# Feed-forward input projection: one pass of 512 columns per rounded weight tile, with the second half copied out by ScalarE

## The reference, cut to what matters

```
h   = rms_norm(x, norm_ffn_g)
a, b = split(h @ ffn_w_in)          # 1024 x (2 * 2816)
x   = x + (silu(a) * b) @ ffn_w_out # 2816 x 1024
```

## Time and profile before

| | |
|---|---|
| median of three runs | 1561.72 us (1561.06 to 1565.51) |
| profiled execution, its span | 1557.4 us |
| median less span | 4.3 us |
| instructions | 28378 |
| busy: TensorE, VectorE, ScalarE | 98%, 76%, 49% of the span |
| share of the closing chain on TensorE | 85% |
| input projection, first to last matmul | 291.2 to 418.3 us |

### The profile page before, as it was taken

The page is one execution under the profiler, slowest core; times in us unless marked ns, Lnnn a source line. Parts: engine busy times, 40 slices in busy tenths (PEclk is TensorE's granted clock), DMA queues, the critical chain, the costliest instruction groups (busy, mean ns, idle before and its releaser), DMA issues.

```text
span 1557.4 us, 28378 instructions
## 1 busy us (share of the span) xinstructions
PE 1530.9 (98%) x10460; PEld 1384.1 (89%) x10460; DVE 1180.4 (76%) x2029; ACT 766.8 (49%) x1089; POOL 60.5 (4%) x108
## 2 busy tenths in 40 slices
PE   8999999999999999999999999999999999999997
PEld 7768897999999887989999999999998888888886
DVE  7996645776636968757699999988865777777776
ACT  5237544544435563425444654645545445444544
POOL 2002000100000034000000000000000000000000
PEclk9999999999999999999999999999999999999999
DMA  7363668455533230516287777555557777777773
GB/s 303 115 259 137 243 241 314 155 184 190 186 112 114 83 109 9 200 49 244 86 228 219 226 225 216 173 165 153 164 157 245 236 239 240 237 242 237 240 243 123
DMA packets 95940, 293.64 MB, mean 189 GB/s; under 512 B 10480, under 2 KB 45424, under 8 KB 82928
## 3 DMA queue, kind: packets, MB, share of 16 engines
q1 hardware_dynamic: 95712, 292.21, 57.1%
q10 hardware_dynamic: 144, 0.26, 0.0%
HBM read 274.60 MB, written 17.83 MB: 188 GB/s over the span
## 4 chain that ended last, share of the span: by engine, by line
PE 85%; DVE 9%; DMA 2%; ACT 1%; issue 1%; SPq 0%; DVEq 0%; POOL 0%; ACTq 0%; POOLq 0%
PE ps L467 85%; DVE big L1518 1%; DVE split_ring L2120 1%; DMA ring<-in_peer_v 1%; DVE big L1543 1%; DMA ring<-in_peer_u 1%; DMA kept_acts<-acts 1%; DVE big L1425 0%; DVE big L2169 0%; DVE big L2173 0%; DVE big L2171 0%; DMA kept_acts<-par 0%; DVE big L1981 0%; DMA x<-in_x 0%; DVE big L1501 0%
## 5 line engine op out<-in xcount | busy, mean ns | idle before, releaser
L467 PE MATMUL ps<-split_hh,split_ring 128*128 128x256 f32 x3392 | 423.2, 284 | 3.6 <-DVE split_ring L2120 3.0
L467 PEld LDWEIGHTS ps<-split_hh,split_ring 128*128 128x128 f32 x3392 | 412.0, 192 | 5.7 <-DVE split_ring L2120 2.3
L467 PE MATMUL ps<-split_ring 128*128 128x512 f32 (+1 forms) x1712 | 386.9, 384 | 3.0 <-DVE split_ring L2120 2.7
L467 PEld LDWEIGHTS ps<-split_ring 128*128 128x128 f32 x1712 | 313.4, 188 | 69.0 <-DVE split_ring L2120 6.6
L2120 DVE TENSOR_TENSOR split_ring<-ring,split_ring 128x1024 fp32r<-128x1024 f32 x256 | 311.7, 1220 | 49.4 <-ACT split_ring L2720 47.3
L2727 ACT ACTIVATE split_ring<-ring 128x1024 fp32r<-128x1024 f32 x128 | 135.8, 1062 | 172.2 <-DMA ring<-in_peer_v 172.1
L2720 ACT ACTIVATE split_ring<-ring 128x1024 fp32r<-128x1024 f32 x128 | 135.2, 1057 | 93.9 <-DMA ring<-in_peer_u 93.8
L467 PE MATMUL ps<-split_ffn_h,split_ffn_w 128*128 128x256 f32 x1056 | 127.4, 283 | 0.0
L467 PEld LDWEIGHTS ps<-split_ffn_h,split_ffn_w 128*128 128x128 f32 x1056 | 127.0, 192 | 0.1
L2229 DVE TENSOR_TENSOR split_ring<-ring,split_ring 128x256 fp32r<-128x256 f32 x128 | 54.4, 425 | 80.4 <-ACT split_ring L2734 80.3
L1726 DVE TENSOR_TENSOR split_ffn_w<-ring,split_ffn_w 128x2048 fp32r<-128x2048 f32 x33 | 75.6, 2291 | 49.8 <-ACT split_ffn_w L2520 49.8
(11 more groups left out here) (348 smaller groups left out, 1895.1 us busy)
## 6 DMA issues: line engine op xcount, KB each, us to landing
ring<-in_peer_u SPq DMA_DIRECT2D x128, 512.0 KB, 4.1
ring<-in_peer_v SPq DMA_DIRECT2D x128, 512.0 KB, 3.6
ring<-in_w_mod SPq DMA_DIRECT2D x24, 1024.0 KB, 5.9
ring<-in_ffn_in SPq DMA_DIRECT2D x22, 1024.0 KB, 4.9
ring<-kept_acts SPq DMA_DIRECT2D x128, 128.0 KB, 3.3
ring<-in_ffn_out SPq DMA_DIRECT2D x11, 1024.0 KB, 4.9
ring<-in_w_out SPq DMA_DIRECT2D x8, 1024.0 KB, 9.0
ring<-in_peer_wq SPq DMA_DIRECT2D x8, 1024.0 KB, 7.6
```

The source lines that it names most:

```text
L467: return nc.tensor.matmul(out, lhsT, rhs, start=start, stop=stop, skip_group_check=True)
```

## The change

Blocks 1 to 21 have one pass of 512 columns where two passes of 256 stood. The rounded weights move `split["ffn_h"][:, :, k, :]`, the high and the low part of the input side by side; the low weights still move the high part alone, into the left 256 columns. Gate and value get a bank each, blocks alternate between bank pairs 0, 1 and 2, 3 outside the planner's turn, and each block waits for block `j - 2` to be taken. The right halves (high weights by low input) are copied to SBUF by ScalarE (`copy_right`), then VectorE adds left and copy, then multiplies by the inverse. Block 0 keeps its 48 matmuls of 256. `ctx_sum` goes to an upper bank, with `after("ctx_sum")` behind it on TensorE, and its square root is placed at the end of ScalarE's turn 1.

```
+        right = h[:, 0:4, :].rearrange("p (n m) t -> p n m t", m=2)
...
+        def ffn_banks(j):
+
+            return ps[:, 2 * (j % 2):2 * (j % 2) + 2, :]
...
-            def total(key, parts, takers=("act",), n=T, ones_=None):
-
-                bank = begin(key, *takers)
+            def total(key, parts, takers=("act",), n=T, ones_=None, upper=0):
+
+                bank = begin(key, *takers, upper=upper)
...
             for j in range(FB):
-                bank = begin(("ffn", j), "dve")
+                if j >= 2:
+                    after(("ffn", j - 2))
+                for b in (2 * (j % 2), 2 * (j % 2) + 1):
+                    if j < 2 and plan.in_bank[b] is not None:
+                        after(plan.in_bank[b])
+                    plan.in_bank[b] = ("ffn", j)
+                plan.add(("ffn", j), ("act", "dve") if j else ("dve",), banked=False)
+                both = ffn_banks(j)
                 weights("ffn_in", j)
                 high, low = (w[:, j % 3, :].rearrange("p (m k c) -> p m k c", m=2, k=KD) for w in (fw_high, fw_low))
                 pe.wait_ge(w_split, len(first_items) + j + 1)
...
+                if j == 0:
...
+                else:
                     for m in range(2):
                         for k in range(KD):
-                            if j == 0 and n == 0 and m == 0:
-                                pe.wait_ge(flag("ffn_h_high_ready"), k + 1)
-                            last = mm(bank[:, m * T:(m + 1) * T], w[:, m, k, :], rhs[:, k, :],
-                                      n == 0 and m == 0 and k == 0, n == 2 and k == KD - 1)
+                            mm(both[:, m, :], high[:, m, k, :], split["ffn_h"][:, :, k, :], k == 0, False)
+                        for k in range(KD):
+                            last = mm(both[:, m, 0:T], low[:, m, k, :], fh_high[:, k, :], False, k == KD - 1)
                 last.then_inc(made, 1)
                 release()
                 if j == 1:
                     pe.wait_ge(flag("squares_folded"), 1)
-                    total("ctx_sum", [sq[:, 0, :]])
+                    total("ctx_sum", [sq[:, 0, :]], upper=1)
+                    after("ctx_sum")
...
             for j in range(FB):
-                bank = s.product(("ffn", j))
                 both = f_both[:, j % 2]
-                s.took(("ffn", j), v.tensor_tensor(both, bank.rearrange("p (a t) -> p a t", a=2), both_r, ALU.mult))
+                dve.wait_ge(made, number(("ffn", j)))
+                left = ffn_banks(j)[:, :, 0:T]
+                if j:
+                    s.after(("ffn", j), "act")
+                    s.took(("ffn", j), v.tensor_tensor(both, left, right[:, j % 2], ALU.add))
+                    s.after(("ffn", j), "dve")
+                    v.tensor_tensor(both, both, both_r, ALU.mult).then_inc(flag("ffn_normed"), 1)
+                else:
+                    last = v.tensor_tensor(both, left, both_r, ALU.mult)
+                    s.took(("ffn", j), last)
+                    s.after(("ffn", j), "dve")
                 if j:
                     hidden_low(j - 1)
                 ffn_low(j + 3)
...
+            def copy_right(j):
+
+                if j == 1:
+                    s.wait("ffn_h_split")
+                if j >= 3:
+                    s.after(("ffn", j - 2), "dve")
+                act.wait_ge(made, number(("ffn", j)))
+                s.took(("ffn", j), a_(right[:, j % 2], ffn_banks(j)[:, :, T:], ACT.Copy))
+
             for j in range(FB):
-                if j == 2:
-                    std_of("ctx_sum", D, T, 1)
                 ffn_high(j + 3)
-                s.after(("ffn", j), "dve")
+                if j:
+                    s.wait("ffn_normed", j)
+                else:
+                    s.after(("ffn", j), "dve")
                 gate = f_both[:, j % 2, 0, :]
                 a_(gate, gate, ACT.Silu).then_inc(flag("silu_ready"), 1)
                 s.wait("hid_ready", j + 1)
                 a_(hid_high[:, j, :], hid[:, j, :], ACT.Copy).then_inc(flag("hid_high_ready"), 1)
+                if j == 1:
+                    std_of("ctx_sum", D, T, 1)
+                if j + 1 < FB:
+                    copy_right(j + 1)
```

More of the change, by code:

```diff
@@ L891, in _ @@
                 pe.wait_ge(w_split, len(first_items) + j + 1)
-                for n, (w, rhs) in enumerate(((high, fh_high), (low, fh_high), (high, fh_low))):
-                    if j == 0 and n == 2:
-                        pe.wait_ge(flag("ffn_h_split"), 1)
+                if j == 0:
+                    for n, (w, rhs) in enumerate(((high, fh_high), (low, fh_high), (high, fh_low))):
+                        if n == 2:
+                            pe.wait_ge(flag("ffn_h_split"), 1)
+                        for m in range(2):
+                            for k in range(KD):
+                                if n == 0 and m == 0:
+                                    pe.wait_ge(flag("ffn_h_high_ready"), k + 1)
+                                last = mm(both[:, m, 0:T], w[:, m, k, :], rhs[:, k, :], n == 0 and k == 0,
+                                          n == 2 and k == KD - 1)
+                else:
                     for m in range(2):
                         for k in range(KD):
-                            if j == 0 and n == 0 and m == 0:
-                                pe.wait_ge(flag("ffn_h_high_ready"), k + 1)
-                            last = mm(bank[:, m * T:(m + 1) * T], w[:, m, k, :], rhs[:, k, :],
-                                      n == 0 and m == 0 and k == 0, n == 2 and k == KD - 1)
+                            mm(both[:, m, :], high[:, m, k, :], split["ffn_h"][:, :, k, :], k == 0, False)
+                        for k in range(KD):
+                            last = mm(both[:, m, 0:T], low[:, m, k, :], fh_high[:, k, :], False, k == KD - 1)
                 last.then_inc(made, 1)
```

## The result

The changed kernel takes 1569.81 us at the median of seven runs (1567.15 to 1572.45), against 1561.72 for the kernel before (seven runs, 1559.98 to 1565.51). The ratio is 1.0044, 95% interval 1.0031 to 1.0057: slower, by 8.1 us (0.44%) between the medians. The profiled execution is the fastest of the seven, 1567.15 us, with a span of 1565.2, 7.8 above the span before.

What follows compares the result with a forecast made beforehand. The prediction took TensorE, busy 98% of the span, as the bound. Its terms, 1.7 + 7.4 + 1.7 + 2.3 - 4.3 = +8.8 us, took the span from 1557.4 to 1566.2; plus 4.3 gave 1570.5 us, range 1565.8 to 1575.5.

Steps and rivals of the forecast that it cites:

- wait before block 0: Before the projection, TensorE waits for ScalarE to take `ffn_sum` from bank 0: 1.7 us more.
- wait behind `ctx_sum`: After block 1, TensorE waits for ScalarE's square root of `ctx_sum`, at the end of its turn 1: 7.4 us more.
- clock behind it: After the `ctx_sum` wait, TensorE's first matmuls run slow, priced like the kernel's start: 1.7 us more, bounds 0 and 3.4.
- wait behind block 4: Block 7 waits for VectorE to take block 5, delayed by its 7.52 us norm of `ctx`: 2.3 us more.
- wide pass: Blocks 1 to 21: 512-column matmuls at 227.3 ns replace pairs at 240.0, saving 4.3 us; bounds 0 and 9.0.
- The 4.3 us put on top of the span: Whole kernel: the median of the runs was taken to stand 4.3 us above the profiled span.
- The rival in which the clock stays up: Behind the `ctx_sum` wait, no slow matmuls: 1.7 us less, 1568.8 us; chance 0.14.
- The two rivals on it, nothing and 9.0 us: Projection blocks 1 to 21: wide pass saves nothing, 1574.8 us, chance 0.08; or saves 9.0 us, 1565.8 us, chance 0.06.
- The loop: Projection's cycle of copy, rounding, low weights, hidden product and rounding: 5.43 us a turn, just under TensorE's 5.56.
- the rival that makes it the bound: From block 8 on, the copy, rounding and hidden-product loop sets the pace: 1571.8 to 1573.7 us; chance 0.14.

Runs made afterwards that it cites:

- the filler: Changed kernel with 31, then 15, float32 matmuls that nobody reads put into TensorE's wait behind `ctx_sum`; 1578.60 and 1572.99 us, one run each.
- the run with two copies: Kernel with all three waits gone, but ScalarE does each copy of a right half twice; 1560.22 us, one run, stage 128.26 us.
- 15 fillers: Changed kernel with 15 float32 matmuls that nobody reads behind `ctx_sum`, ending before the square root; 1572.99 us, one run.
- 31 fillers: Changed kernel with 31 float32 matmuls that nobody reads behind `ctx_sum`, running past the square root's end; 1578.60 us, one run.
- the kernel with the narrow passes: Kernel with all three waits gone, but each wide pass undone into two of 256 columns, copy and add kept; 1562.13 us, ratio to before 0.9996.

## Why the prediction was right

The time, 1569.81, lies in the range, 0.7 us under the forecast of 1570.5, and slower as forecast. Term by term, with the runs' values in the stage:

| term | forecast, us | measured, us | from |
|---|---|---|---|
| wait before block 0 | +1.7 | +1.72 | start of the projection, 2.50 after the sum against 0.78 |
| wait behind `ctx_sum` | +7.4 | +7.36 | 312.08 - 304.48 less 0.24 before (303.14 - 302.90) |
| clock behind it | +1.7 | +1.96 | block 2's copy, 7.92 against 5.96 us |
| wait behind block 4 | +2.3 | +2.08 | first matmuls of blocks 6 and 8, 349.82 - 336.56, less two blocks of 5.59 |
| block 0's own matmuls | none | -0.09 | 5.85 against 5.94 us, by first matmuls |
| wide pass | -4.3 | -3.63 | stage of 124.48 against 128.11 |
| sum | +8.8 | +9.40 | the stage, measured whole: +9.38 |

That the time came nearer to its forecast than this sum did is in part luck. The stage was 0.6 us longer than forecast, while the work behind it took 1.7 us less than before in the profiled execution (1137.2 against 1138.9), which no run traces to the change. The 4.3 us put on top of the span is no fixed cost either: the changed kernel's profiled run took 1.9 us more than its span (1567.15 against 1565.2), and the rest of the 4.6 us up to its median is that this run was the fastest of seven.

*The waits.* All three stood where the prediction put them, ended by the instructions it named. The walk through the times was good to 0.1 us for the first two, because each of their steps was in the trace of before: TensorE ran past the same square roots there, and their ends could be read off. The third is 0.2 us short of the forecast, since TensorE is ready for block 7 that much later. The prediction let block 0 of the kernel before last 5.76 us and so had ScalarE begin 0.45 us after the end of a block; by the first matmuls block 0 lasted 5.94 us (to 297.14), and ScalarE began 0.26 us after it. The rest is that a block takes 5.59 and not 5.56 us.

*The clock.* I had read the lower level from the pace of the first matmuls after the start, against a granted clock of 1.00 in the earlier trace rows. In the changed kernel the column itself shows 0.50 behind the long wait, and the filler takes the fall away. Its price, 1.96 us, is near the 1.7 borrowed from the start, but it is not fixed: with the bank pairs swapped the same wait was followed by a block 2 that was 0.6 us faster. The rival in which the clock stays up is refuted for this wait. The Trainium skill, "TensorE: Matmul & The Clock Gate", part 1, "The HAM clock gate", has the throttled state as default with activity as its release; the stretches of 0.50 after the wait and of 1.00 with the filler agree.

*The wide pass.* Mis-sized by 0.7 us: the term used 227.3 ns for a wide matmul and 240.0 for a pair, 12.7 saved; the runs give 10.8, a wide matmul of 229.2 ns. The two rivals on it, nothing and 9.0 us, are both refuted. By the Trainium skill, "TensorE: Matmul & The Clock Gate", "Back-to-back issue gap", whose formula is for a matmul by itself, the change would have saved 2.5 ns a pair; the measurement decides for 10.8.

*The loop.* Back to back it takes 353.44 - 348.03 = 5.41 us in the changed kernel, where 5.43 was forecast (copies of blocks 6 and 7):

```profile
348.03 0.58 ACT L2575 ACTIVATE hh<-ps 128x512 f32<-128x512 f32 x1
...
353.44 0.58 ACT L2575 ACTIVATE hh<-ps 128x512 f32<-128x512 f32 x1
```

It stays 0.18 us under TensorE's block, so the rival that makes it the bound did not come in; the run with two copies shows that it would have, and at the place and price that its arithmetic gives.

*Where it was less sure than it looked.* The prediction added up one profile. The three waits stood in every profile that has them, but the clock's falls did not (below), and the forecast had only one. The waits removed one by one give back 8.5, 2.2 and 2.1 us, 12.8 in all; the three together 13.0. The parts nearly add up.

## What to carry to other kernels

A product that is taken out late costs nothing while nobody needs its bank, and everything once the busiest engine waits for it by name: before placing a wait on that engine, read from the trace when the thing waited for ends, and ask whether a later wait already covers it. With fewer banks in rotation a long block of work on the draining engine, here one norm of 7.5 us, can become a gap on TensorE. Widening the moving operand is worth its 10.8 ns a pair only where these waits are kept off; with them gone the same change is 0.41% faster than the kernel before, of which the stage shows 3.63 us, 0.23%.

## What the runs showed that I had not expected

Short waits can drop TensorE's clock too, and not in every execution. In the profile of the changed kernel neither the gap of 1.37 us before block 0 nor that of 1.87 before block 7 did, the granted clock stayed at 1.00. With 15 fillers both were followed by 0.50 to 0.74, and with 31 fillers the gap of 1.86 us before block 7 was:

```profile
349.00:352.00 3.00, 2.27 (x7) 1.90 (x8) 2.97 (x5) 0.42 (x1) 0.00 (x0) 0.77 0.86 322
352.00:356.00 4.00, 4.00 (x19) 3.47 (x18) 2.93 (x6) 2.75 (x4) 0.00 (x0) 0.75 0.04 14
```

The length of the gap alone does not decide it: in the kernel without the wait behind `ctx_sum` the gap of 2.68 us before block 7 was longer than any of these, and the granted clock stayed at 1.00 behind it. What decides whether a short gap is followed by a fall stays open.

The seven runs of the changed kernel have mean granted clocks of 0.993 to 0.997, the slowest run the lowest and the fastest the highest, and spread over 5.3 us. That these falls make the spread is not shown: the kernel before, which has none of the three waits, spread over 5.5 us in its seven runs, and the kernel with the narrow passes, which has none either, over 6.3 us in eleven.
